# Time tables, norm factors in two parts, a shared scaling and earlier loads in a two-block transformer kernel

## The reference

```python
def first_block(x, ...):
    z = rms_norm(h, attn_norm) @ w_in
    o_nsa = nsa_mixer(...)      # 8 heads of 64, 2 groups of keys: compressed, selected and window attention,
                                # each gated; with 8 blocks of 64 and top_k 8 the selected one is plain causal attention
    o_gla = gla_mixer(...)      # gated linear attention, 4 heads: log_a = log_sigmoid(..)/16, cumsum per chunk of 64,
                                # state = decay * state + dS, o = rms_norm(o) * silu(g_out)
    h = h + concatenate([o_nsa, o_gla]) @ w_out
    u = causal_dwconv(rms_norm(h) @ w_up)
    h = h + (silu(gate) * up) @ w_down

def second_block(h, ...):       # 16 meta tokens ahead of the 512
    proj = rmsnorm(h) @ w_in
    q, k = l2norm(silu(conv(dq))), l2norm(silu(conv(dk)));  v = silu(conv(dv))
    g = -exp(a_log) * softplus(da + dt_bias);  beta = sigmoid(db)
    o_dn = rmsnorm(gated_delta_rule(q, k, v, g, beta), dn_gain) * silu(dz)      # 8 heads, 128 x 256, chunks of 64
    o_sb = stick_breaking_attention(rmsnorm(sq), rmsnorm(sk), sv)               # 8 heads of 128
    merged = sigmoid(gate_dn) * (o_dn @ w_branch_dn) + sigmoid(gate_sb) * (o_sb @ w_branch_sb)
    h = h + merged @ w_out
    h = h + swiglu(rmsnorm(h))
```

## Time and profile before

| | |
|---|---|
| median of 3 runs | 2288.2 us (2282.61 to 2294.2) |
| profiled execution | 2287.53 us |
| its span | 2285.7 us |
| mean granted clock of PE | 0.98 |
| PE busy | 2201.2 us, 96% |
| PEld busy | 1704.8 us, 75% |
| DVE busy | 1114.9 us, 49% |
| ACT busy | 800.9 us, 35% |
| POOL busy | 68.6 us, 3% |
| DMA | 214.46 MB, 94 GB/s on average |

### The profile page before, as it was taken

The page is one execution under the profiler, slowest core; times in us unless marked ns, Lnnn a source line. Parts: engine busy times, 40 slices in busy tenths (PEclk is TensorE's granted clock), DMA queues, the critical chain, the costliest instruction groups (busy, mean ns, idle before and its releaser), DMA issues. The chain is left out here.

```text
span 2285.7 us, 32675 instructions
## 1 busy us (share of the span) xinstructions
PE 2201.2 (96%) x13572; PEld 1704.8 (75%) x13572; DVE 1114.9 (49%) x1800; ACT 800.9 (35%) x1306; POOL 68.6 (3%) x88
## 2 busy tenths in 40 slices
PE   8999789999999899989999999999999999999999
PEld 7776456888888898976766888767566678888887
DVE  3464675777742467654435534346433254444422
ACT  3332454444432443332214222225346443222211
POOL 0000002000000000000000000000012101000000
PEclk9999899999999999989999999999999999999999
DMA  4124001222222243332124421115621032222322
GB/s 166 60 74 148 10 2 65 93 92 92 94 99 93 79 146 127 122 103 70 57 71 158 136 85 66 62 56 185 218 78 51 20 119 93 92 92 93 101 92 92
DMA packets 76291, 214.46 MB, mean 94 GB/s; under 512 B 8432, under 2 KB 12912, under 8 KB 76144
## 3 DMA queue, kind: packets, MB, share of 16 engines
q1 hardware_dynamic: 76144, 212.37, 27.7%
HBM read 183.64 MB, written 27.66 MB: 92 GB/s over the span
## 5 line engine op out<-in xcount | busy, mean ns | idle before, releaser
L296 PE MATMUL ps<-nx_hi,whi 128*128 128x264 f32 (+1 forms) x1504 | 539.1, 358 | 13.1 <-DVE nx_lo L385 9.7
L274 ACT ACTIVATE whi<-raw 128x1024 fp32r<-128x1024 f32 x282 | 298.7, 1059 | 632.5 <-PE ps L298 442.3
L281 DVE TENSOR_TENSOR wlo<-raw,whi 128x1024 fp32r<-128x1024 f32 x282 | 346.1, 1227 | 346.8 <-ACT whi L274 346.7
L298 PE MATMUL ps<-nx_hi,wlo 128*128 128x264 f32 (+1 forms) x1504 | 512.6, 341 | 0.0
L297 PE MATMUL ps<-nx_lo,whi 128*128 128x264 f32 (+1 forms) x1504 | 512.4, 341 | 0.0
L296 PEld LDWEIGHTS ps<-nx_hi,whi 128*128 128x128 f32 x1504 | 287.5, 191 | 79.5 <-issue 45.6
L298 PEld LDWEIGHTS ps<-nx_hi,wlo 128*128 128x128 f32 x1504 | 287.5, 191 | 32.4
L297 PEld LDWEIGHTS ps<-nx_lo,whi 128*128 128x128 f32 x1504 | 288.2, 192 | 30.2 <-issue 1.9
L298 PE MATMUL ps<-x_hi,wlo 128*128 128x512 f32 x528 | 209.6, 397 | 0.0
L297 PE MATMUL ps<-x_lo,whi 128*128 128x512 f32 x528 | 208.3, 395 | 0.0
L296 PE MATMUL ps<-x_hi,whi 128*128 128x512 f32 x528 | 208.0, 394 | 0.0
(11 more groups left out here) (463 smaller groups left out, 2859.2 us busy)
## 6 DMA issues: line engine op xcount, KB each, us to landing
raw<-stream_dram SPq DMA_DIRECT2D x285, 512.0 KB, 3.5
qk_spill<-ring SPq DMA_DIRECT2D x16, 264.0 KB, 2.2
qk_cols<-qk_spill SPq DMA_DIRECT2D x16, 264.0 KB, 4.2
v_spill<-ring SPq DMA_DIRECT2D x16, 264.0 KB, 2.1
v_cols<-v_spill SPq DMA_DIRECT2D x16, 264.0 KB, 4.2
dz_spill<-ring SPq DMA_DIRECT2D x16, 256.0 KB, 2.1
dz<-dz_spill SPq DMA_DIRECT2D x16, 256.0 KB, 5.7
sbk_spill<-ring SPq DMA_DIRECT2D x8, 264.0 KB, 2.1
```

The lines of the kernel that those rows point to most:

```text
L274: act.activation(K.whi[:, n % HL], K.raw[:, n % RAW], ACT.Copy).then_inc(K.s_hi, 1)
L281: dve.tensor_tensor(K.wlo[:, n % HL], K.raw[:, n % RAW], K.whi[:, n % HL].bitcast(F32), ALU.subtract).then_inc(K.s_lo, 1)
L296: pe.matmul(out, whi, xhi, start=start, stop=False, skip_group_check=skip)
L298: return pe.matmul(out, wlo, xhi, start=False, stop=stop, skip_group_check=skip)
```

## The change

Four kinds of edits:

1. Time tables. Numbers that place `Linear`, `Gates`, `NormCols` and `DeltaOutput` among the dense products change.
2. Norm factors in two parts. `NormCols` makes its factors as an fp32r part and a remainder (DVE: reciprocal, a scaled copy, a remainder) and spreads them with two fp32r matmuls against a column of an fp32r identity over 128 rows, two halves each, where an fp32 matmul over 32 rows stood. ACT zeroes the unused rows and copies the identity behind the first square.
3. First attention. PE issues the scores of unit u + 2 before it transposes unit u. DVE scales the first head of a unit, GpSimd the second. Four slots hold maxima, sums and factors, and the weights take turns in two buffers of two units. DVE takes one maximum ahead of the factors and one behind, ACT the exponentials before its copy. The casts of identity and mask stand in the stage before.
4. Loads. In the three stages whose first chunk is begun early, the raw chunk that takes its slot is asked for at the end of the stage before.

```diff
 # out_ffn, Products.sp and SecondBranch.sp leave out their first load when begun; Begun does it:
+    def sp(self, sp):
+        yield 1e6
+        if self.first + HL < self.K.n_stream:
+            load_chunk(self.K, sp, self.first + HL)
 # Gates: PE (g), DVE (g), DVE (g_cum), DVE (beta exp g), ACT
-        yield self.at(0.5)      +        yield self.at(0.75)
-        yield self.at(0.45)     +        yield self.at(0.62)
-        yield self.at(0.65)     +        yield self.at(0.85)
-        yield self.at(1.0)      +        yield self.at(1.05)
-        yield self.at(0.8)      +        yield self.at(0.92)
 # NormCols
-        return self.t0 + (self.spread_time(0) - 2 * self.step - self.t0) * i / n
+        return self.t0 + (self.spread_time(0) - 4 * self.step - self.t0) * i / n
-            yield self.square_time(i) - 4 * self.step
+            yield self.square_time(i) - (self.step if self.ready is not None else 1.8)
+            if i == 0:
+                none = cst(K, "ones")[64:P, 0:1].broadcast_to([64, HALF])
+                act.activation(self.rt_hi[64:P], none, ACT.Copy, scale=0.0)
+                act.activation(self.rt_lo[64:P], none, ACT.Copy, scale=0.0)
+                act.activation(self.ident[:], cst(K, "ident"), ACT.Copy).then_inc(z["n_ident"], 1)
-        yield self.spread_time(0) - 1.5 * self.step
+        yield self.spread_time(0) - 3.5 * self.step
-                mm = pe.matmul(K.ps[:, self.pairs[i % len(self.pairs)] + h, 0:e - a],
-                               cst(K, "ident")[32 * h:32 * h + 32, 32 * h + i:32 * h + i + 1].broadcast_to([32, P]),
-                               self.rt[32 * h:32 * h + 32, 0:e - a], start=True, stop=True)
+                pe.matmul(out, row, self.rt_hi[:, 0:e - a], start=True, stop=False)
+                mm = pe.matmul(out, row, self.rt_lo[:, 0:e - a], start=False, stop=True)
-        yield self.spread_time(0) - self.step
+        yield self.spread_time(0) - 3 * self.step
-        dve.tensor_scalar(self.rt[:], self.rt[:], cst(K, self.scales, 64), None, ALU.mult).then_inc(z["n_factors"], 1)
+        K.dve_chain.link(dve, dve.tensor_scalar(self.rt_hi[0:64], self.rt[:], by, None, ALU.mult))
+        scaled_lo(dve, self.rt[:], by, self.rt_hi[0:64], self.rt_lo[0:64]).then_inc(z["n_factors"], 1)
 # DeltaOutput: units and first transposes
-        return self.at(0.5 + i / 16)
+        return self.at(0.545 + 0.056 * i)
-                            yield self.at(0.43 + 0.0125 * m)
+                            yield self.at(0.47 + 0.0125 * m)
 # Linear: log_a on DVE, and the table
-        yield t_["cum"] - 0.2
+        yield t_["cum"] - 0.7
-            times = dict(logits=5.3, cum=6.6, kd_t=8.6, states=9.9, out=10.9, step=0.8, norm=14.6, o_t=16.4)
+            times = dict(logits=5.3, cum=7.2, kd_t=9.3, states=10.5, out=11.2, step=0.8, norm=14.6, o_t=16.4)
 # the three NormCols: first square, end, step
-                             "dn_scales", (2, 4), z, c3, 5, 16, 0.25, free=(z["gate_made"], 1)),
+                             "dn_scales", (2, 4), z, c3, 6.4, 16, 0.28, free=(z["gate_made"], 1)),
-                                  "dn_scales", (0,), z, c3, 1.0, 8, 0.3),
+                                  "dn_scales", (0,), z, c3, 2.2, 8, 0.3),
-                                     "sb_scales", (2, 4), z, c3, 0.4, 8, 0.2, fetched=8),
+                                     "sb_scales", (2, 4), z, c3, 0.6, 8, 0.19, fetched=8),
 # nsa_attend, PE
-                        pe.wait_ge(s_w, 2 * u + a + 1)
+                        pe.wait_ge((s_fc, s_w)[a], u + 1)
                 for u in range(NU):
+                    scores(u + 2)
                     transposed(u)
-                    scores(u + 2)
                     values(u - 1)
 # nsa_attend, DVE: weights() becomes factors(), with one scaling
-                    for a in range(2):
-                        p = pr[:, u % 2, a, 0:(t + 1) * P]
-                        dve.tensor_scalar(p, p, fc[:, u % 2, a:a + 1], None, ALU.mult).then_inc(s_w, 1)
+                    p = probs(u, 0, (t + 1) * P)
+                    dve.tensor_scalar(p, p, fc[:, u % 4, 0:1], None, ALU.mult).then_inc(s_fc, 1)
                 for u in range(NU):
-                    weights(u + 1)
                     maximum(u + 2, 0)
+                    factors(u + 1)
+                    maximum(u + 2, 1)
                     dve.wait_ge(s_tr, 2 * u + 2)
                     dve.tensor_copy(pt[:, u % 2, 1, 0:(units[u][1] + 1) * P],
                                     K.ps[:, 5, 0:(units[u][1] + 1) * P]).then_inc(s_pt1, 1)
-                    maximum(u + 2, 1)
 # nsa_attend, GpSimd
+            @block.gpsimd
+            def _(pool):
+                for u in range(NU):
+                    pool.wait_ge(s_fc, u + 1)
+                    p = probs(u, 1, (units[u][1] + 1) * P)
+                    pool.tensor_scalar(p, p, fc[:, u % 4, 1:2], None, ALU.mult).then_inc(s_w, 1)
```

More of the change, by code:

```diff
@@ L425, in _ @@
             def _(sp):
-                load_chunks(K, sp, first, n_all)
+                early = 0 if begun is None else 1
+                load_chunks(K, sp, first + early, n_all - early)
                 for d in store:
@@ L801, in sp @@
             yield self.at(c / self.n)
-            if self.first + c + HL < self.K.n_stream:
+            if self.first + c + HL < self.K.n_stream and not (c == 0 and self.begun is not None):
                 load_chunk(self.K, sp, self.first + c + HL)
@@ L1765, in pe @@
                 u = 2 * j + f
-                yield self.unit(2 * u - 2) if u else self.at(0.43)
+                yield self.unit(2 * u - 2) if u else self.at(0.47)
                 if u >= 2:
@@ L2783, in dve @@
         ch.link(dve, dve.memset(tb[:], 0.0))
+        dve.tensor_copy(R.ident16[:], cst(K, "ident"))
+        dve.tensor_copy(R.causal16[:], cst(K, "causal"))
         yield t_["cmp"] - 0.3
@@ L2876, in nsa_attend @@
 def nsa_attend(K, R):
-    s_sc, s_mx, s_ex, s_w, s_tr, s_pt0, s_pt1, s_pv, s_oh, s_oc, s_masks = sems(
-        K, "scores", "maxima", "probs", "weighted", "transposed", "even_t", "odd_t", "pv", "o_hi", "o_copied", "masks")
+    s_sc, s_mx, s_ex, s_fc, s_w, s_tr, s_pt0, s_pt1, s_pv, s_oh, s_oc = sems(
+        K, "scores", "maxima", "probs", "factors", "weighted", "transposed", "even_t", "odd_t", "pv", "o_hi", "o_copied")
     rows = R.rows.rearrange("p (g t c) -> p g t c", g=4, t=TT)
@@ L2888, in nsa_attend, with probs @@
     with ExitStack() as c:
[L2889 to L2891 removed]
+        pr0, pt, pr1 = [R.rows[:, 2048 * g:2048 * g + 2048].rearrange("p (u a n) -> p u a n", u=2, a=2) for g in (0, 2, 3)]
+        mx, sm, fc = [scratch(K, c, n, [P, 4, 2]) for n in ("max", "sum", "factor")]
+        def probs(u, a, ext):
+            return (pr0, pr1)[u // 2 % 2][:, u % 2, a, 0:ext]
         with K.nc.Block() as block:
@@ L2955, in maximum, with factors @@
                         dve.wait_ge(s_sc, 2 * u + a + 1)
-                        dve.tensor_reduce(mx[:, u % 2, a:a + 1], K.ps[:, 2 * (u % 2) + a, 0:(units[u][1] + 1) * P], AX.X, ALU.max,
+                        dve.tensor_reduce(mx[:, u % 4, a:a + 1], K.ps[:, 2 * (u % 2) + a, 0:(units[u][1] + 1) * P], AX.X, ALU.max,
                                           negate=True).then_inc(s_mx, 1)
-                def weights(u):
+                def factors(u):
                     if u >= NU:
@@ L2981, in _ @@
                         maximum(u, a)
-                weights(0)
+                factors(0)
                 for u in range(NU):
-                    weights(u + 1)
                     maximum(u + 2, 0)
+                    factors(u + 1)
+                    maximum(u + 2, 1)
                     dve.wait_ge(s_tr, 2 * u + 2)
```

43 lines of the change are left out of this document (24 added, 19 removed).

## The result

| | before | changed |
|---|---|---|
| median | 2284.05 us (6 runs) | 2264.06 us (6 runs) |
| lowest to highest | 2280.33 to 2294.2 | 2262.97 to 2273.1 |
| ratio, 95% interval | | 0.9916 [0.99, 0.9932] |
| span of the profiled execution | 2285.7 | 2261.3 |
| mean granted clock | 0.980 | 0.981 |

The kernel is faster by 0.84%, 20 us between the medians and 24.4 between the two profiled spans. The forecast was 2262 in 2240 to 2280, worked out as 25.1 us less than the profiled execution of before.

What follows compares the result with a forecast made beforehand. TensorE (PE) was taken as the bound, its waits and clock dips as what edits could shorten. Terms of -3.7, -1, -11, -1.2, -0.5, +6, -2, -1.7 and -10 sum to -25.1 from 2287.5: about 2262 us, range 2240 to 2280.

Steps and rivals of the forecast that it cites:

- A: Linear attention's time table: PE's wait for log_a shrinks, the clock dip may go, new waits come; -3.7 us (+1 to -6).
- G: First attention's new order with GpSimd scaling: the cover just suffices, waits for DVE and mask casts go; -10 us (-2 to -13).
- D: Squares in the first DeltaOutput stage: PE waits 7.5 us behind a weight split whose chunk lands late; +6 us (0 to +11).
- B: Gates moved past the wait charged to g: 0.6 us gained, pause and dip stay; -1 us (0 to -5).
- C: Norm factor spreads in two parts: 0.25 to 0.35 us saved per tile for 32 tiles, -11; first norm stage's waits -1.2.
- Third norm stage: Third norm stage: some waits for squares shrink, -0.5 us, and its cheaper spreads bring -5.6.
- F: Raw loads a stage ahead in three stages: a 1.7 us wait goes in the last branch, nothing elsewhere; -1.7 us.
- E: Second DeltaOutput stage: PE reaches the first transposes 2.1 us later, leaving 3.1 us of waits; -2 us (0 to -5.2).

## Why the prediction was right

The time came out 2 us from the forecast, and the signs of the parts too. The gain itself is 20.0 us by medians and 24.4 by profiles, for 25.1: part of the closeness is that the forecast started from 2287.5, where the median of before is 2284.05 in these runs. And two of the terms, A and G, are short by 4.5 us together, while dips gave 2.3 in stages that nobody changed and 1.7 in the second DeltaOutput stage. That they made up for one another is luck.

- **D, the squares.** Computed: 36 products, arrival 8.6 us into the stage, a wait of 7.5; measured 8.6 and 7.8, and the stage +2.9 with the spreads' share, forecast +3.2. The cause (a raw chunk behind dz on a full queue, ahead of the square on ACT) is shown for 4.9 of the 7.8 by the kernel with later dz loads, in which that split waits no more.
- **B, the gates.** "The pause stays": 3.85 us, and without the table loads it is gone. What the gates' new table brought by itself no run separates.
- **A, the table of the linear attention.** Forecast -3.7, measured -2.0. The wait shrank as computed (0.6, said 0.7) and new ones came (1.6 and 1.4, said 1.7 and 0.7), but the step that failed is "With it the dip may go", priced at -3.4: the dip behind log_a went, and one came at 123 us. With the old table the kernel is 3.4 us faster than the change by medians, so nothing of A is shown to be the table's worth.
- **C, the spreads.** 0.84 to 0.49 us per tile holds on PE (0.48), and the third norm stage shows it (0.32 a tile). The sum of 11 was too much: undoing the spreads costs 7.4 by medians and 9.2 by profiles, 2.4 of the latter through dips. The step that failed is "for 32 tiles": in two of three stages DVE paces the spreads, and 16 tiles bring 0.11 each.
- **Third norm stage.** -6.1, as forecast, but not only for the reasons given: F's "In the other two PE waited for nothing of the kind" holds for the kernel before, but not once the rest is changed: without the early loads a split of this stage waits for its load, and the stage is 2.6 us longer.
- **G, first attention.** -7.2 for -10, and -8.9 without the dip behind it, which the forecast didn't have. The other mis-sized term is GpSimd's scaling, 0.6 to 1.57 us where 0.35 to 0.9 was taken, outside the 0.3 to 1.0 that was to show it; the pairs, at 21.86, are under the 22.2 that was. But the wait that replaced the old ones was not for GpSimd, it was for ACT's copy behind two exponentials, which stands in the changed order and which the prediction passed over. And the floor was wrong: it took the 21.6 us busy per pair as what PE needs, and PE needs 20.08 at most. No run undoes the new order of the scores by itself.
- **E and F.** -3.5 for -2: the wait is 3.3, as computed (3.1), and the dip behind it shrank from 6.8 to 3.4 us, 1.7 that weren't forecast. And -2.1 for -1.7 in the last branch, of which undoing the loads gives back 0.8.
- Unchanged stages moved by -2.3 us, through a dip of 3.4 us at 1338 where before there were 10.2 at 1347. A single profile can't tell parts under about 3 us.

## What to carry to other kernels

Where a table moves an instruction, look at what now stands ahead of it on each of its engines, and at the load behind that: the wait of 7.8 us could be computed from the order and three rows. Before pricing a wait as gained, ask what holds the engine named, and what is late next; in the first attention that was a copy that stood behind work nobody waited for yet, worth 5.8 us in the stage (10 between the medians, dips included) for one moved call. Don't take PE's busy time as its need where matmuls are short. And set the marks that divide a trace into stages on the engine that bounds the kernel.

## What the runs showed of the hardware

- GpSimd's tensor_scalar with a per-partition factor takes 0.605, 0.925, 1.245 and 1.565 us for 128, 256, 384 and 512 fp32 columns, 0.32 per 128; by a constant 0.530 to 1.547 (at 512 columns 1.49, or 1.72 in two of eight, beside a VectorE scaling). Its copy of 128 columns took 0.293.
- An ACT table load took 1.28 us each. A weight split behind four in a row made PE stop for 3.9 us, and without them it didn't stop.
- The same wait of 3.4 us for log_a was followed by 6.8 us at half clock in one execution (before, 67.38 to 74.20) and by 3.4 us in another (the old table back, 69.30 to 72.71). A wait of 2.7 us near 194 was followed by 6.8 us before, by 3.4 in the changed kernel and by none with the old table back. So a dip's price differs between kernels whose instructions there are the same.
- A VectorE scaling and a GpSimd one that overlap cost one of the two 0.2 to 0.4 us in six of the seven overlaps of more than 0.15 us, in the kernel with GpSimd's work doubled.
